# Order of RWKV's work and form of the norms in a kernel of three transformer layers

## What is computed

```python
def rms_norm(x, g):
    y = xf * lax.rsqrt(jnp.mean(xf * xf, axis=-1, keepdims=True) + NORM_EPS)
    return (y * g).astype(x.dtype)

for l in range(2):                                   # first block
    h = rms_norm(x, norm_mix_g) * (1 + sc_m) + sh_m  # sc, sh, g: modulation, silu(c) @ ada_w + ada_b
    proj = h @ w_in                                  # neighbourhood, MLA and GQA attention from it
    merged = sigmoid(ga) * (o_na @ w_br_na) + sigmoid(gb) * (o_mla @ w_br_mla) + sigmoid(gc) * (o_gqa @ w_br_gqa)
    x = x + g_m * (merged @ w_out)
    h = rms_norm(x, norm_ffn_g) * (1 + sc_f) + sh_f
    gate, up = jnp.split(h @ ffn_w_gate_up, 2, axis=-1)
    x = x + g_f * ((silu(gate) * up) @ ffn_w_down)
x = rms_norm(x, final_norm_g)

h = rms_norm_2(x, norm1_g)                           # second block
pa, pb, pg, pc = _split(h @ w_in, (COLS_A, COLS_B, COLS_GATE, COLS_C))
y_a = b_a * causal_dwconv(c_a * x_a, conv_a_w)
y_b = rg_lru(causal_dwconv(x_b, ...), ...) * gelu(g_b)
r, k, v, xw, xa, xg = _split(token_shift(pc, mu), ...)
decay = exp(-exp(-softplus(-(w0 + tanh(xw) @ w2)) - 0.5))
a = sigmoid(a0 + xa @ a2);  g_c = sigmoid(xg) @ g2
kk = k * rwkv_kk;  kk = kk / maximum(sqrt(sum(kk * kk)), 1e-12)      # per head of 64
k = k * (1 + (a - 1) * ka)
state = state * w_t + (state @ -kk_t) (kk_t * a_t)^T + v_t k_t^T;  y_t = state @ r_t
y_c = ((y normalised per head) * lnx_g + lnx_b + sum(r * k * r_k) * v) * g_c
m = gate_a * y_a + gate_b * y_b + gate_c * y_c
x = x + m @ w_out
x = x + square(relu(rms_norm_2(x, norm2_g) @ mlp_w1)) @ mlp_w2
return rms_norm_2(x, final_g)
```

## Time and profile before

| what | us |
|---|---|
| median of three runs (lowest, highest) | 3298.68 (3297.34, 3301.64) |
| profiled execution | 3296.89 |
| its span, first to last instruction | 3295.1 |
| TensorE, VectorE, ScalarE, GpSimd busy | 3022.4, 1778.6, 660.3, 1277.1 |
| granted TensorE clock, mean over the span | 0.960 |

### The profile page before, as it was taken

One profiled execution on the slowest core, in us unless ns is written; L12 is line 12 of the kernel. 1 busy time (PEld: TensorE's weight loads), 2 busy tenths in 40 slices (PEclk: granted clock), 3 DMA queues, 4 the chain that ended last, 5 costly groups with the idle time before them and its releaser, 6 DMA issues.

```text
span 3295.1 us, 43929 instructions
## 1 busy us (share of the span) xinstructions
PE 3022.4 (92%) x17988; PEld 2315.5 (70%) x17988; DVE 1778.6 (54%) x2301; ACT 660.3 (20%) x1126; POOL 1277.1 (39%) x940
## 2 busy tenths in 40 slices
PE   3999888999989999989999798998998998989998
PEld 2766666778767667768888476776776776768886
DVE  6678765666245665354432565565555556364252
ACT  1343211000003432010000322322322312210000
POOL 1323334455543233535555222323323323335553
PEclk8999999999989999989999799999999999989999
DMA  9535566577753234545555223323323323345553
GB/s 297 174 126 176 198 197 212 172 241 239 230 168 138 75 114 135 169 141 193 195 197 206 91 87 107 109 87 103 112 81 108 108 81 108 115 140 191 191 191 115
DMA packets 174628, 503.79 MB, mean 153 GB/s; under 512 B 41206, under 2 KB 56566, under 8 KB 174198
## 3 DMA queue, kind: packets, MB, share of 16 engines
q1 hardware_dynamic: 82800, 274.75, 25.8%
q0 software_dynamic: 67392, 218.40, 18.7%
q10 hardware_dynamic: 24262, 8.21, 1.5%
HBM read 280.76 MB, written 6.06 MB: 87 GB/s over the span
## 4 chain that ended last, share of the span: by engine, by line
PE 76%; DVE 12%; DMA 4%; issue 3%; POOL 3%; ACT 1%; SPq 0%; ACTq 0%; DVEq 0%; POOLq 0%
PE ps L324 21%; PE ps L326 20%; PE ps L325 20%; PE ps L1117 4%; DMA raw<-in_weights_dram 4%; PE ps L969 2%; POOL wR L527 2%; PE ps L979 2%; PE ps L989 1%; DVE hR L1358 1%; DVE work L1352 1%; DVE work L1747 1%; PE ps L1127 1%; DVE hR L1356 1%; DVE rB L1693 1%
## 5 line engine op out<-in xcount | busy, mean ns | idle before, releaser
L324 PE MATMUL ps<-hR,wR 128*128 128x512 f32 x2320 | 981.8, 423 | 85.1 <-DVE hR L1358 44.2
L527 POOL TENSOR_TENSOR wR<-raw,wR 128x1024 fp32r<-128x1024 f32 (+3 forms) x468 | 1014.1, 2167 | 77.9 <-DMA wR<-raw 68.3
L518 POOL DMA_DIRECT2D wR<-raw x468 | 266.2, 569 | 1905.3 <-issue 1466.2
L326 PE MATMUL ps<-hR,wR 128*128 128x512 f32 x2320 | 922.1, 397 | 0.0
L325 PE MATMUL ps<-hR,wR 128*128 128x512 f32 x2320 | 921.8, 397 | 0.0
L324 PEld LDWEIGHTS ps<-hR,wR 128*128 128x128 f32 x2320 | 447.1, 193 | 247.6 <-issue 77.8
L326 PEld LDWEIGHTS ps<-hR,wR 128*128 128x128 f32 x2320 | 445.4, 192 | 98.3
L325 PEld LDWEIGHTS ps<-hR,wR 128*128 128x128 f32 x2320 | 448.4, 193 | 93.2 <-issue 13.1
L1315 DVE CUSTOM_DVE_ANT_0 raw<-raw,cs 128x1024 f32<-128x1024 f32 x96 | 162.0, 1696 | 64.2 <-DMA raw<-in_weights_dram 57.8
L1364 DVE SCALAR_TENSOR_TENSOR xT<-ps,lm,xT 128x512 f32<-128x512 f32 x32 | 24.0, 751 | 243.2 <-PE ps L326 243.2
L324 PE MATMUL ps<-act_f,wR 128*128 128x512 f32 x352 | 139.4, 396 | 2.3 <-POOL wR L527 2.3
(11 more groups left out here) (337 smaller groups left out, 4237.7 us busy)
## 6 DMA issues: line engine op xcount, KB each, us to landing
raw<-in_weights_dram SPq DMA_DIRECT2D x490, 512.0 KB, 3.3
wR<-raw POOLq DMA_DIRECT2D x394, 512.0 KB, 2.9
raw<-in_weights_dram SPq DMA_DIRECT2D x50, 128.0 KB, 2.5
wR<-raw POOLq DMA_DIRECT2D x50, 128.0 KB, 2.0
raw<-in_weights_dram SPq DMA_DIRECT2D x16, 256.0 KB, 3.7
wR<-raw POOLq DMA_DIRECT2D x16, 256.0 KB, 3.3
bias_toeplitz<-bias_rows ACTq DMA_DIRECT2D x8, 476.2 KB, 17.2
bias<-bias_toeplitz ACTq DMA_DIRECT2D x16, 224.0 KB, 6.8
```

The source lines that it names most:

```text
L324: mm(out, w_hi, r_hi, start=first, stop=False)
L326: return mm(out, w_lo, r_hi, start=False, stop=last)
L518: pool.dma_start(wR[:, u, 0, 0:cols], raw[:, r % RING, 0:cols]).then_inc(hi_ready[u], 16)
L527: nc.gpsimd.tensor_tensor(wR[:, u, 1, 0:cols], raw[:, r % RING, 0:cols], wR[:, u, 0, 0:cols], ALU.subtract).then_inc(tile_ready, 1)
```

## The change

In the norms:

- `product` one and two become `pair_of_products`: for each step k, three matmuls of one and three of the other, so both wait for h in turn and both claim their bank at once. This holds for both mixes' first two tiles, both FFNs, the two `B2` products and both halves of the MLP. The loops behind start one round later.
- ScalarE does the rounding (`round_h`, Identity with bias) between VectorE's two remaining operations.
- The seventh square is added ahead of the last residual, and the sum over `tmp` (`first_sums`) is issued inside the last product, ahead of its last step; `last_sums` adds the last square.
- Between the blocks one pass serves both norms: ScalarE makes a second set of squares scaled by the gain, VectorE keeps two sums (`add_both`, in `tmp` and `hf`), TensorE sums both (banks `SUM` and `OB`), and the second root follows from the first. x itself is multiplied only behind `vec2_ready`, ahead of RWKV's tile 0.
- In `RAW` weight tiles 0 and 1 move ahead of the last modulation rows of the first sixteen.
- `turn(0)`, `turn(1)` move one product later.

In RWKV:

- w, a, g stand ahead of r. The sum of k's squares for tile m+1 is issued behind v(m+1) at the end of tile m; VectorE takes the maximum in the middle of `finish` (`floor_k`), and ScalarE takes Ln and Exp (`root_k`) in place of a square root and VectorE's reciprocal.
- On VectorE r's shift and bnB go behind `prep_ready`; kB's, rB's scaling and the bonus product go behind the T sums of levels 1, 2 and 3. The bonus sum moves into level 2, bank `SUM`.
- TensorE fills 21 steps ahead of the block products, 7 behind them, then 3 in levels 1 and 2, 4 ahead of the chunks (before: 27, 4, 2 and 1, 2).
- `lru_scale` and `conv_in` change places; `centre` and the square go ahead of g1.

The core of the diff:

```diff
     for m in range(KD):
+        small(("w", "a", "g"), m, 0)
         full("r", m)
-        small(("w", "a", "g"), m, 0)
...
 RAW = [("mod", j) for j in range(N_FIRST)]
+RAW.insert(N_FIRST - 1, ("tile", 1))
+RAW.insert(N_FIRST - 3, ("tile", 0))
...
+            def round_h(H, shift):
+                for k in range(KD):
+                    full = (tmp, hf)[k % 2]
+                    act.wait_ge(full_ready, H + k + 1)
+                    A(hR[:, 0, k, :], full, ACT.Identity, bias=lm[:, shift + k:shift + k + 1]).then_inc(h_rounded, 1)
...
                 norm(Count(Q), Count(R), Count(PR - KD))
+                round_h(2 * KD * l, SH_M)
                 act.wait_ge(s_rows, 32 + 64 * (l + 1))
...
+            def root_k(m):
+                act.wait_ge(kk_floor, m + 1)
+                A(rt, rt, ACT.Ln).then_inc(log_ready, 1)
+                logs.append(m)
+                act.wait_ge(log_ready, len(logs))
+                act.wait_ge(root_used, R0 + 2 + 2 * m)
+                A(rs, rt, ACT.Exp, scale=-0.5).then_inc(root_ready, 1)
...
-                act.wait_ge(shifted, 5 * m + 1)
-                take_shift("r", m, 0, rB[:], W_MUR)
                 take("w", m, e1[:, :, 0:P], ACT.Tanh, bias=vec(half2, W_W0), scale=0.5)
                 take("a", m, aB[:], ACT.Tanh, bias=vec(half2, W_A0), scale=0.5)
+                root_k(m)
                 act.wait_ge(m_done, m + 1)
                 take("g", m, gB[:])
-                root(Count(Q0 + 8 + 2 * m), Count(R0 + 1 + 2 * m), 1, 1)
                 act.wait_ge(d_ready, m + 1)
                 A(e1[:], dB[:], ACT.Exp, scale=-RATE / 2)
                 A(e2[:], dB[:], ACT.Exp, scale=RATE / 2).then_inc(e_ready, 1)
+                act.wait_ge(shifted, 5 * m + 1)
+                take_shift("r", m, 0, rB[:], W_MUR)
...
+            def pair_of_products(ts, p, H):
+                slots, banks = [need_tile(Count(t)) for t in ts], [claim(Count(p + j)) for j in range(2)]
+                for k in range(KD):
+                    pe.wait_ge(h_ready, H + k + 1)
+                    for j in range(2):
+                        mm = three_passes(MM, ps[:, banks[j], :], weight(slots[j], 0, k * P), weight(slots[j], 1, k * P),
+                                          h_hi(k), h_lo(k), k == 0, k == KD - 1)
+                        if k == KD - 1:
+                            mm.then_inc(tile_used, 1)
...
+                        if u == KD - 1 and k == KD - 1:
+                            first_sums(R + 5, 2 * l + 1)
...
+                            if u == KD - 1 and k == KF - 1:
+                                first_sums(R_LAYER * (l + 1), 2 * (l + 1))
+                                if l == DEPTH - 1:
+                                    MM(ps[:, OB, :], ones[:], hf, start=True, stop=False)
...
+            sum_tile(Q0 + 8, R0 + 1)
             for m in range(KD):
-                fill(14)
-                sum_tile(Q0 + 8 + 2 * m, R0 + 1 + 2 * m)
-                fill(13)
+                fill(21)
...
-                while mix_at() < (MIDX["r", m + 1] if m < KD - 1 else len(MIX)):
+                while mix_at() < (MIDX["w", m + 1] if m < KD - 1 else len(MIX)):
                     fill(1)
+                if m < KD - 1:
+                    sum_tile(Q0 + 10 + 2 * m, R0 + 3 + 2 * m)
...
+            def norm(H, scale, shift, inv=None):
+                for k in range(KD + 1):
+                    if k < KD:
+                        if k >= 2:
+                            dve.wait_ge(h_ready, H + k - 1)
+                        V.scalar_tensor_tensor((tmp, hf)[k % 2], xT[:, k, :], gs[:, scale, k:k + 1], rs if inv is None else inv,
+                                               ALU.mult, ALU.mult).then_inc(full_ready, 1)
+                    if k == KD - 1:
+                        dve.wait_ge(full_ready, H + KD)
+                        dve.sem_inc(root_used, 1)
+                    if k:
+                        dve.wait_ge(h_rounded, H + k)
+                        V.scalar_tensor_tensor(hR[:, 1, k - 1, :], (tmp, hf)[(k - 1) % 2], lm[:, shift + k - 1:shift + k], hR[:, 0, k - 1, :],
+                                               ALU.add, ALU.subtract).then_inc(h_ready, 1)
...
+            for k in range(KD):
+                v(STT(xT[:, k, :], xT[:, k, :], vecx[:, X_F1 + k:X_F1 + k + 1], rs, ALU.mult, ALU.mult))
...
+            def floor_k(m):
+                dve.wait_ge(sq_used, (Count(Q0 + 8 + 2 * m) + (1 + C_UNIT)).value())
+                TS(rt, ps[:, SUM, :], 1e-24, None, ALU.max).then_inc(kk_floor, 1)
...
                 v(TT(yB[:], yB[:], gB[:], ALU.mult))
+                if m < KD - 1:
+                    floor_k(m + 1)
...
-                v(TS(rs, rt, 1e-12, None, ALU.max))
-                v.sync()
-                v(V.reciprocal(rs, rs))
...
+                    if lv == 1:
+                        v(TT(decay[:, 0:CH - 1], e1[:, 0:CH - 1, P], e2[:, 1:CH, 0], ALU.mult))
+                        dve.wait_ge(bn_in, m + 1)
+                        TT(ch(kB[:]), ch(kB[:]), e2[:, :, 1:P + 1], ALU.mult).then_inc(k_scaled, 1)
+                    elif lv == 2:
                         dve.wait_ge(uhi_ready, m + 1)
                         TT(uR[:, 1, :], hf, uR[:, 0, :], ALU.subtract).then_inc(u_ready, 1)
+                        TT(ch(rB[:]), ch(rB[:]), e1[:, :, 1:P + 1], ALU.mult).then_inc(r_scaled, 1)
```

More of the change, by code:

```diff
@@ L997, in fill @@
                         next(work_left, None)
-                for p in range(FIRST):
+                pair_of_products((TI, TI + 1), PR, H)
+                for p in range(2, FIRST):
                     fill(8)
-                    if p in (1, 2):
-                        turn(p - 1)
+                    if p < 4:
+                        turn(p - 2)
                 for s in range(STEPS_ATT):
@@ L1613, in _ @@
             v.sync()
-            take_root(Count(R0 - 1))
-            for k in range(KD):
-                STT(xT[:, k, :], xT[:, k, :], vecx[:, X_F1 + k:X_F1 + k + 1], rs, ALU.mult, ALU.mult).then_inc(xf_ready, 1)
-            dve.wait_ge(xf_ready, KD)
-            dve.sem_inc(root_used, 1)
-            norm(Count(R0), Count(H0), 0, 0)
+            dve.wait_ge(var_ready, 1)
+            TT(hf, ps[:, OB, :], tmp, ALU.mult).then_inc(var_ready, 1)
+            take_root(Count(R0))
+            v(TT(rt, rs, tmp, ALU.mult))
+            v.sync()
+            norm(H0, 0, 0, rt)
             dve.wait_ge(s_in2, 64)
@@ L1867, in _ @@
                 lru_gate()
-                conv_in()
+                lru_scale()
                 for cc in range(CH - 1):
```

205 lines of the change are left out of this document (119 added, 86 removed).

## The result

The changed kernel takes 3193.1 us (median of four; 3187.2 to 3194.4) against 3298.2 for the kernel before on the same chip: a ratio of 0.9676, 95% interval 0.9659 to 0.9693. The forecast was 3169 with a range of 3140 to 3210: right in sign and in that range, but 24 us too low at the point and 3 us outside the narrower 3150 to 3190 to which 0.60 was given. The number lies nearest to that of rival D (3197), which did not come; only the trace tells them apart. The profiled execution of after took 3187.2 around a span of 3185.4, that of before 3296.9 around 3295.1; between these two, 109.7 us went where the sum says 129.4.

What follows compares the result with a forecast made beforehand. TensorE, busy 92% of the span, left only idle and slow time to gain. First norm +16, RWKV tiles -98, the other norms' savings and MLP +2.4 summed to -129.4: 3298.7 to 3169 us, range 3140 to 3210.

Steps and rivals of the forecast that it cites:

- rival D: The paired products behind the norms stay at the low clock, 4 x 7 us more, 3197 us; chance 0.09.
- What goes from a tile: In each RWKV tile, TensorE stalls of 10.0 us and 4.4 us of low clock vanish, together 14.4 us.
- Step (e): Centring ahead of g1, square ahead of its tanh: the stall at the sum of squares goes, otherwise 3.51 us again.
- (c): root_k's Ln and table load on ScalarE finish before they are wanted: nothing, 1.3 us if that cover is gone.
- (d): VectorE's added work behind the T sums of levels 1 to 3: 0, or up to 2.4 us a tile.
- (f): conv_in goes behind the first state update: TensorE's wait at L1211, 6.2 us in total, goes.
- What comes in its place: New stall ahead of a tile's block products, VectorE's chain with three GpSimd collisions: 1.7 us taken, ends 0 and 5.2.
- The tail: From tile 7's block products to norm 2's first h: -13.1 us, with 8.7 for the last tile's tail.
- The norms: Last product to first h -4.4 us where GpSimd hit; FFN pairs -6.8 each, norm 2's -5.0; double norm -18.
- Rival C: ScalarE's DMA issues in the first norm cost TensorE nothing, 3150 us; chance 0.13.
- B: The stall ahead of the RWKV block products stays, 5 us and 2.2 of low clock a tile, 3213 us; chance 0.16.
- E: Slower than before: the wait for k's sum holds up VectorE's chain beyond 34 us in RWKV tiles; chance 0.02.

Runs made afterwards that it cites:

- the run with short subtractions: Changed kernel with GpSimd's subtraction cut to 32 columns for the RWKV tiles' weights, part of the products left out: 3151.7 us, ratio 0.9552.
- the shorter chain: Changed kernel with finish's last four operations behind kkB, and kB's product, bnB and r's shift moved into level 1: 3187.3 us, ratio 0.9646.
- the run with all together: The shorter chain plus DMA order, double norm edits, sp chain inside tile 0 and no pair in the MLP's second half: 3156.4 us, ratio 0.9558.

## Why the prediction was right or wrong

**What goes from a tile** (14.4 us): right, 14.7 by the run with short subtractions. Step (e) was 4.9 instead of 5.4. Steps (c), (d) and (f) cost nothing, as forecast: root_k was through at V + 7.1, and nobody waits between the levels or for the state.

**What comes in its place** (1.7 us): this is the step that failed, and with it -98. The chain without collisions was V + 11.4 in the text and V + 11.2 on the chip; the error is the count of collisions, "3 x 2.4 = 7.2", taken from the products of v, the small tile and r. There were four, 8.9 us. The fourth is xb's: a chain that ends at the text's own V + 18.6 is still running when xb's product has ended, and that subtraction started at V + 16.0 (2099.36) and fell on L1850. (The text also took L1717 for an operation with two inputs; it has one, and is hit all the same.) The count follows from the rate: a product takes 5.44 us and brings one subtraction of 2.4, so a chain of VectorE's own work advances 3.0 us in 5.4. 11.4 - 1.3 of own work behind floor_k then take about 18 us: V + 19.4, near the V + 20.4 measured. From floor_k to kkB the same share gives 18.3 us for the changed kernel's own 10.2, 13.6 for the 7.6 with the rest of finish moved and 12.5 for the 7.0 of the shorter chain; measured were 19.1, 14.0 and 13.0. And of the 2.5 us between its own V + 18.6 and V + 16.1 the text took 1.7; 4.0 stood there. In all, 4.7 us came in the place of what went (112.9 - 108.2): by the rows of the six tiles above 4.1 of it is idle time of TensorE and 0.5 longer busy time. r's bank was freed at V + 16.4 and wanted at V + 14.8, as forecast (16.7, 15).

**The tail.** 7.3 instead of 13.1. Behind tile 7's block products TensorE has 162 matmuls with h where before it had 144: the change moves six steps of dense work behind them, 18 x 0.227 = 4.1 us, which the sum has left out. The rest, 1.7, fits the 3 us or so at half the clock behind the wait of 2.53 us there, which I had counted as gone.

**The norms.** The sum was good (FFN 1 with mix 2 -15.7 for -11.2, FFN 2 with the double norm -28.3 for -29.2), its reasons only partly. From last product to first h: 8.0 us for 8.6. From first h to product three: 14.2 for 15.1 (13.3 and 0.9 of emptying, for 13.5 and 1.6), but most of the gain is ScalarE's rounding (0.72 us, no table load among them; I took 0.65). Behind the double norm the hole for the emptying is 5.7 as forecast (6.0), k's sum waits 7.2, not 4: the eight scalings took 10.03 us instead of 5.4, GpSimd again. Its first h came 13.9 us behind the last product, not 15.7, which paid for part of that.

**The first norm.** Right: product three at 89.40 (87 to 92), +13.9 for +16. With some luck: in the eight other executions with ScalarE's DMAs in this order it starts at 89.9 to 93.7, in seven of them later than 92, behind a hole of 13.0 to 17.9 us. Rival C is out: with eight DMAs split and four moved the hole is gone. That it isn't won back was right in the changed kernel (merge at 533.2 against 519.7).

**Rivals B, D, E.** B, the old stall whole (5 us and 2.2 of clock), did not come, though its cause did: it was 4.0 us, and no low clock but in tile 7. D did not come: behind FFN 2's first h the clock is 0.67 over 6.8 us and 1.00 from there. Nothing of E: over all runs floor_k waits at most 3.0 us in tile 0 and 2.04 in the others.

## What to carry to other kernels

Where GpSimd works in step with the products, don't count which of VectorE's operations it hits: price VectorE's chain at the share of time that GpSimd leaves (here 3.0 in 5.4), and shorten the chain rather than reorder it. An operation taken off a path must land where the idle time is longer than itself and one collision, or it comes back as another wait; four operations moved in one piece gained nothing, one by one, with two small edits that made room for them, they gave 3.5 us a tile over the run with all together. A wait has two prices, its length and the clock behind it: merging two short ones into one long one cost 1.8 us a tile at the same total.

## What the runs showed of the hardware

The granted clock behind a wait, all ahead of the block products: 1.00 behind 2.38 to 2.51 us with one of 1.6 us shortly before it, low for some 3 us behind 2.53 in tile 7, but 1.00 behind all seven in the run with the DMAs in another order, 2.54 among them; 0.50 to 0.63 over 4 us behind 2.76 in seven tiles; 0.50 for 3.8 us behind 4.22. Yet in the run without pairs three of seven tiles with the same 2.4 us had some 3 slow us behind them (114.2 us instead of 112.8), and tile 7 again: near this length the wait alone doesn't decide it.

VectorE was held up by GpSimd's subtraction in operations on SBUF alone, also one with a single input (2.72 us instead of 0.43) and even a copy of 128 x 4 elements (2.71 instead of 0.17, in the run with the shorter chain):

```profile
2104.02 2.71 DVE L1840 COPY mid<-dB 128x4 f32<-128x4 f32 x1
```

An operation that reads PSUM and one constant passed in 0.68. In the Trainium skill, "SBUF — State Buffer", "Who interferes with whom", copies and tensor-scalar operations in a two-port mode contend as those with two SBUF inputs do. The rows fit that, though no run here shows in which mode they ran. In the hits counted above the price was between 1.57 us (L1811) and 2.71 (L1784 with finish ahead of floor_k) beside subtractions of 2.4, and it didn't follow the size of VectorE's operation: the small copy paid 2.54.

How long ScalarE's DMA issues take depends on the moment: the same eight took 18.72 us at 45 us and 7.94 at 70 (7.8 to 9.5 in nine executions); the four others 11.12 before, 10.3 to 13.8 in nine executions behind those eight, and 6.28 when they were issued at 45 us in an idle queue. No run separates what sets it.
